# Four tiles of a product taken from the scaled input, with the norm's root multiplied in afterwards

## The reference

```python
def rmsnorm(x, g):
    xf = x.astype(jnp.float32)
    y = xf * lax.rsqrt(jnp.mean(xf * xf, axis=-1, keepdims=True) + RMS_EPS)
    return (y * g.astype(jnp.float32)).astype(x.dtype)

def modulate(h, shift, scale):
    return h * (1 + scale) + shift
...
        hx = modulate(rmsnorm(x, norm_g[l]), shift[:, None], scale[:, None])
...
def odd_mixer(h, p, on_grid):
    z = h @ p["w_in"]
    u, g = jnp.split(z, [W_POOL], axis=-1)
    d = multiscale_pool(u.reshape(bn * rows, GRID_W, W_POOL)).reshape(bn, n, W_POOL)
    d = d.reshape(bn, n, N_POOL_GROUPS, POOL_GROUP_DIM)
    y = jnp.einsum("bngi,gij->bngj", d, p["w_grp"]).reshape(bn, n, W_POOL) * p["scale"]
    return (y * jax.nn.silu(g)) @ p["w_out"]
```

## Time and profile before

| | us |
|---|---|
| median of 3 runs | 910.2 (910.13 to 910.39) |
| the profiled execution | 910.26 |
| its span in the trace | 908.5 |
| PE busy | 889.2 (98% of the span) |
| DVE busy | 700.0 (77%) |
| ACT busy | 500.7 (55%) |
| POOL busy | 142.5 (16%) |

### The profile page before, as it was taken

One profiled execution on the slowest core, in us unless ns is written; L12 is line 12 of the kernel. 1 busy time (PEld: TensorE's weight loads), 2 busy tenths in 40 slices (PEclk: granted clock), 3 DMA queues, 4 the chain that ended last, 5 costly groups with the idle time before them and its releaser, 6 DMA issues.

```text
span 908.5 us, 17445 instructions
## 1 busy us (share of the span) xinstructions
PE 889.2 (98%) x7172; PEld 834.4 (92%) x7172; DVE 700.0 (77%) x1008; ACT 500.7 (55%) x718; POOL 142.5 (16%) x254
## 2 busy tenths in 40 slices
PE   8999999999999999999999999999999999999996
PEld 7788776689999999989999999999999999999995
DVE  5689667989897999978579975797985688656553
ACT  5384888897744455325554474574444444444441
POOL 0003874800021002300211100300001000000000
PEclk9999999999999999999999999999999999999999
DMA  9946987885675777866628844555565386666661
GB/s 365 385 142 219 310 266 227 271 281 178 210 275 198 254 266 262 292 216 190 183 84 319 283 139 140 192 153 180 172 183 171 123 267 209 183 182 178 202 202 54
DMA packets 55294, 195.44 MB, mean 215 GB/s; under 512 B 7856, under 2 KB 7984, under 8 KB 53808
## 3 DMA queue, kind: packets, MB, share of 16 engines
q1 hardware_dynamic: 39600, 147.73, 50.6%
q0 software_dynamic: 15616, 46.61, 14.9%
HBM read 188.60 MB, written 1.05 MB: 209 GB/s over the span
## 4 chain that ended last, share of the span: by engine, by line
PE 76%; DVE 11%; ACT 5%; DMA 4%; issue 3%; SPq 0%; DVEq 0%; ACTq 0%
PE ps L575 22%; PE ps L577 21%; PE ps L576 21%; PE ps L736 3%; DVE w_lo L1373 3%; DMA raw<-in_stream 2%; PE px L654 2%; DMA m<-in_mod_w 2%; PE ps L665 2%; ACT w_hi L958 1%; DVE win L1387 1%; PE px L841 1%; DVE dump L1744 1%; PE px L816 1%; ACT la L1078 1%
## 5 line engine op out<-in xcount | busy, mean ns | idle before, releaser
L1373 DVE TENSOR_TENSOR w_lo<-raw,w_hi 128x1024 fp32r<-128x1024 f32 x232 | 280.5, 1226 | 103.7 <-ACT w_hi L958 103.1
L958 ACT ACTIVATE w_hi<-raw 128x1024 fp32r<-128x1024 f32 x232 | 243.2, 1056 | 116.1 <-DMA raw<-in_stream 116.0
L575 PE MATMUL ps<-h_hi,w_hi 128*128 128x256 f32 (+1 forms) x928 | 273.9, 295 | 7.1 <-DVE w_lo L1373 2.8
L576 PE MATMUL ps<-h_lo,w_hi 128*128 128x256 f32 (+1 forms) x928 | 269.5, 290 | 0.0
L577 PE MATMUL ps<-h_hi,w_lo 128*128 128x256 f32 (+1 forms) x928 | 269.3, 290 | 0.0
L575 PEld LDWEIGHTS ps<-h_hi,w_hi 128*128 128x128 f32 x928 | 177.6, 191 | 17.6 <-issue 6.4
L576 PEld LDWEIGHTS ps<-h_lo,w_hi 128*128 128x128 f32 x928 | 177.7, 191 | 3.6 <-issue 1.2
L577 PEld LDWEIGHTS ps<-h_hi,w_lo 128*128 128x128 f32 x928 | 177.7, 191 | 2.6
L452 POOL DMA_DIRECT2D modw<-in_mod_w x80 | 42.8, 537 | 384.7 <-DVE modw L1407 242.7
L575 PE MATMUL ps<-h2o_hi,w_hi 128*128 128x256 f32 x352 | 101.5, 288 | 0.0
L577 PE MATMUL ps<-h2o_hi,w_lo 128*128 128x256 f32 x352 | 99.6, 283 | 0.0
(11 more groups left out here) (336 smaller groups left out, 1759.5 us busy)
## 6 DMA issues: line engine op xcount, KB each, us to landing
raw<-in_stream SPq DMA_DIRECT2D x252, 512.0 KB, 4.0
modw<-in_mod_w POOLq DMA_DIRECT2D x80, 512.0 KB, 5.8
m<-in_mod_w SPq DMA_DIRECT2D x8, 1024.0 KB, 19.4
shifts<-upad POOLq DMA_DIRECT2D x128, 35.5 KB, 4.9
c_row<-in_c_rows SPq DMA_DIRECT2D x3, 512.0 KB, 6.3
ctxT<-in_ctxT SPq DMA_DIRECT2D x1, 1024.0 KB, 5.2
x<-in_xT SPq DMA_DIRECT2D x1, 1024.0 KB, 7.2
ctx2T<-in_ctx2T SPq DMA_DIRECT2D x1, 1024.0 KB, 6.6
```

The source lines that it names most:

```text
L575: pe.matmul(o, wh, hi, start=start, stop=False)
L576: pe.matmul(o, wh, lo, start=False, stop=False)
L958: act.activation(w_hi[split[0] % HI_RING][:], raw[n % RING][:], ACT.Copy).then_inc(w_hi_ready, 1)
L1373: v.tensor_tensor(w_lo[n % RING][:], raw[n % RING][:], w_hi[split[0] % HI_RING][:].bitcast(F32), ALU.subtract).then_inc(w_lo_ready, 1)
```

## The change

The first four `ou` tiles no longer wait for the norm. While the `yb` tiles are added to `x`, ACT makes `xa_hi` = x * scale and DVE the rest `xa_lo`, tile by tile. Two more columns of `xa` hold the shift, so a matmul is 258 wide and its column 256 gives the product with the shift. PE multiplies ou 0 to 3 by `xa` one tile after another (`thirds` in place of `side_by_side`), with the two matmuls of the sum of squares between ou 0 and ou 1, and all 18 `keep_busy` matmuls there are gone. Afterwards DVE, for each of the four tiles (`ou_root`), copies column 256 into `sums1` and multiplies the tile by the reciprocal root into `first1`; ACT adds `sums1` on the way into `opad`. ou 4 to 15 and all of `og` use `h1` as before. DVE makes `yb`'s four modulation products together, ahead of `yb` 4, runs two tiles of `w_lo` ahead of its `yb` adds in place of four from `yb` 4 on, and clears the edges of `opad` later.

```diff
--- before.py
+++ after.py
@@ -238,6 +238,9 @@
         win = [at("win0", W + 68, [16, PW]), at("win1", W + 73, [16, PW])]
         y_hi = at("y_hi", W + 78, [16, T], F32R)
         vr1 = at("vr1", W + 94, [T])
+        TS1 = T + 2
+        xa_hi, xa_lo = at("xa_hi", W + 77.75, [KT, TS1], F32R), at("xa_lo", W + 85.875, [KT, TS1], F32R)
+        first1 = at("first1", W + 12, [4, T])
         h1_hi = at("h1_hi", W + 97.25, [KT, T], F32R)
         h1_lo = at("h1_lo", W + 105.25, [KT, T], F32R)
         y_lo = at("y_lo", W + 97.25, [16, T], F32R)
@@ -362,6 +365,7 @@
         act_step = sem("act_step")
         out_done = sem("out_done")
         xg_ready = sem("xg_ready")
+        xa_rounded, xa_ready, first_ou = sem("xa_rounded"), sem("xa_ready"), sem("first_ou")
 
         modA = columns(2 * KT).rearrange("p (k w) -> p k w", w=2)
         modS = columns(2 * KT).rearrange("p (k w) -> p k w", w=2)
@@ -375,6 +379,7 @@
         ccs = columns(2 * KT)
         warm, eps_col = columns(1), columns(1)
         sc1, gate1 = columns(KT), columns(KT)
+        sums1 = columns(4)
         shift1 = columns(KT)
         lb_t = [columns(2 * HEADS) for _ in range(3)]
         lb, oml, noml = (columns(2 * HEADS) for _ in range(3))
@@ -717,13 +722,13 @@
                 thirds("yb", t, *yb, first=False)
 
 
-            keep_busy(4)
-            two_chunks(px[0], sq1, 1, KT)
-            keep_busy(14)
             h1 = (lambda k: h1_hi[:, k, :], lambda k: h1_lo[:, k, :])
-            side_by_side([("ou", t) for t in range(4)], *h1, (h_ready, 0))
+            for t in range(4):
+                thirds("ou", t, lambda k: xa_hi[:, k, :], lambda k: xa_lo[:, k, :], TS1, (xa_ready, 1) if t == 0 else None)
+                if t == 0:
+                    two_chunks(px[0], sq1, 1, KT)
             for t in range(4, 2 * KT):
-                thirds("ou", t, *h1)
+                thirds("ou", t, *h1, ready=(h_ready, 0) if t == 4 else None)
             for t in range(2 * KT):
                 thirds("og", t, *h1)
             two_chunks(px[1], sqx, 2, 2 * KT)
@@ -1188,19 +1193,25 @@
                 act.activation(dst[:, t, :], x[:, t, :], ACT.Square).then_inc(sq_ready, 1)
 
             root_table()
+            act.activation(xa_hi[:, :, T:TS1], shift1.rearrange("p (k a) -> p k a", a=1).to_broadcast([P, KT, 2]), ACT.Copy) \
+               .then_inc(xa_rounded, 1)
             for t in range(KT):
                 done("yb", t)
+                emptied(act, "yb", t)
+                act.activation(xa_hi[:, t, 0:T], x[:, t, :], ACT.Identity, scale=sc1[:, t:t + 1]).then_inc(xa_rounded, 1)
                 squares("yb", t, sq1)
+            highs("ou", 4)
 
             root_of_mean(5, vr1[:], px[0])
             shifted(0, h1_hi, t1, shift1)
+            highs("ou", 6)
             act.wait_ge(pads_ready, 1)
-            highs("ou", 5)
-            for t in range(2 * KT):
-                if t < 4:
-                    act.wait_ge(tile_done, TILE[("ou", t)] + 1)
-                else:
-                    done("ou", t)
+            for t in range(4):
+                emptied(act, "ou", t)
+                act.activation(opad[:, t, :, 8:8 + GRID_W], first1[:, t, :].rearrange("p (r c) -> p r c", c=GRID_W),
+                               ACT.Identity, bias=sums1[:, t:t + 1]).then_inc(first_ou, 1)
+            for t in range(4, 2 * KT):
+                done("ou", t)
                 act.activation(opad[:, t, :, 8:8 + GRID_W],
                                psum_of("ou", t)[:, 0:T].rearrange("p (r c) -> p r c", c=GRID_W), ACT.Copy) \
                    .then_inc(free_of("ou", t), 1)
@@ -1386,9 +1397,9 @@
             def tt_(o, a, b, op):
                 return v.tensor_tensor(o, a, b, op)
 
-            def modulate(count, src, rstd, scale, shift, tmp, hi, lo):
-
-                for s in range(KT + 2):
+            def modulate(count, src, rstd, scale, shift, tmp, hi, lo, steps=range(KT + 2)):
+
+                for s in steps:
                     if s < KT:
                         v.scalar_tensor_tensor(out=tmp[:, s, :], in0=src[:, s, :], scalar=scale[:, s:s + 1], in1=rstd,
                                                op0=ALU.mult, op1=ALU.mult).then_inc(pre_ready, 1)
@@ -1690,17 +1701,28 @@
 
             def add_to_x(name, t, gate):
 
-                if t < KT - 1 or name == "ob":
+                if name != "yb" and (t < KT - 1 or name == "ob"):
                     ahead(name, t)
                 v.wait_ge(tile_done, TILE[(name, t)] + 1)
                 xt = x[:, t, :]
                 v.scalar_tensor_tensor(out=xt, in0=psum_of(name, t)[:, 0:T], scalar=gate[:, t:t + 1],
                                        in1=xt, op0=ALU.mult, op1=ALU.add).then_inc(free_of(name, t), 1)
 
+            v.wait_ge(xa_rounded, 1)
+            v.tensor_tensor(xa_lo[:, :, T:TS1], shift1.rearrange("p (k a) -> p k a", a=1).to_broadcast([P, KT, 2]),
+                            xa_hi[:, :, T:TS1].bitcast(F32), ALU.subtract).then_inc(xa_ready, 1)
             for t in range(KT):
+                if t == 4:
+                    lows("yb", 4)
+                    mod_tiles(7, 1)
+                    lows("yb", 5)
                 add_to_x("yb", t, gate0)
-                if t < 4:
-                    mod_tiles(7, 1, t, 1)
+                if t < KT - 1:
+                    ahead("yb", t, 4 if t < 4 else 2)
+                emptied(v, "yb", t)
+                v.wait_ge(xa_rounded, t + 2)
+                v.scalar_tensor_tensor(out=xa_lo[:, t, 0:T], in0=x[:, t, :], scalar=sc1[:, t:t + 1],
+                                       in1=xa_hi[:, t, 0:T].bitcast(F32), op0=ALU.mult, op1=ALU.subtract).then_inc(xa_ready, 1)
 
             def rstd(n, t, dst):
 
@@ -1710,10 +1732,26 @@
 
 
             lows("ou", 3)
+            rstd(4, vr1[:], vr1[:])
+
+            def ou_root(t):
+
+                v.wait_ge(tile_done, TILE[("ou", t)] + 1)
+                S.do(v.tensor_copy(sums1[:, t:t + 1], psum_of("ou", t)[:, T:T + 1]))
+                S.sync()
+                v.tensor_tensor(first1[:, t, :], psum_of("ou", t)[:, 0:T], vr1[:], ALU.mult).then_inc(free_of("ou", t), 1)
+
+            ou_root(0)
+            modulate(0, x, vr1[:], sc1, shift1, t1, h1_hi, h1_lo, range(4))
+            lows("ou", 4)
+            modulate(0, x, vr1[:], sc1, shift1, t1, h1_hi, h1_lo, range(4, KT + 2))
+            ou_root(1)
+            lows("ou", 5)
+            ou_root(2)
+            ou_root(3)
             S.do(v.memset(opad[:, :, :, 0:8], 0.0))
             v.memset(opad[:, :, :, 8 + GRID_W:PW], 0.0).then_inc(pads_ready, 1)
-            rstd(4, vr1[:], vr1[:])
-            modulate(0, x, vr1[:], sc1, shift1, t1, h1_hi, h1_lo)
+            lows("ou", 6)
             v.wait_ge(pads_ready, 1)
 
             def window(g):
@@ -1760,6 +1798,8 @@
 
             def pooled(g):
 
+                if g == 0:
+                    v.wait_ge(first_ou, 4)
                 for t in range(4 * g, 4 * g + 4):
                     emptied(v, "ou", t)
                 total = window(g)
```

## The result

The changed kernel takes 917.33 us (median of 5, 916.2 to 924.1) against 910.2: a ratio of 1.0082 (95% interval 1.0056 to 1.0108), so 7 us slower. A second series of the same kernel gave 917.45 (12 runs, 915.66 to 924.03) against 910.98 (35 runs, 909.39 to 917.78) for the kernel before, a ratio of 1.0069 (1.0045 to 1.0093), 6.5 us. The forecast was 916.8 within 914.4 to 918.6.

A forecast was written before the change was run, and what follows sets the result against it. DVE's unbroken work from the last add through `w_lo` of ou 7 sets the pace: 6.5 us added, less 0.7 idle, plus 0.8 for the clock makes 6.6 us slower, 916.8 us (914.4 to 918.6).

The forecast's parts named there:

- PE at the border: Between yb 7 and ou 0: ou 0 starts 6.3 us earlier without a wait; seen from PE alone, a 5.3 us gain.
- The yb adds cost nothing: Ahead of the border: extra `xa_lo` and four modulation products in a row cost nothing, covered by PE's 14.4 us.
- Four `ou_root`, 3.1 us: On DVE behind the last add: four copy-and-multiply pairs at 0.77 us each, from a range of 0.55 to 0.85.
- DVE's sum: Work added on DVE between the last add and `w_lo` of ou 7: 6.5 us (5.5 to 6.8).
- The idle time ahead of the second window sum goes: DVE's 0.73 us idle ahead of `pooled(1)` vanishes, so ou 10 starts 6.5 - 0.7 = 5.8 us later.
- The clock, 0.8 of 0.2 to 1.4: PE's clock falls in the wait ahead of ou 7, which starts at half rate: 0.8 us reach the path.
- Waits of 1.5, 0.6 and 8.6: PE's waits for `w_lo`: about 1.5 us for ou 5, 0.6 for ou 6 and 8.6 for ou 7.
- Nothing comes back later: Between 345 and 900 us, later waits take up none of the delay: 0 given back, at best 0.3 us.
- The sum: Whole kernel: 5.8 + 0.8 = 6.6 us slower; profiled execution 916.9 us, median 916.8 us.
- PE's gain arrives: Rival: PE's 5.3 us gain at the border reaches the end, giving 904.9 us; chance 3%.
- DVE's path alone, no clock term: Rival: clock stays at 2.4 GHz through the wait ahead of ou 7 or rises at once; 916.0 us; chance 24%.
- It doesn't do what it says: Rival: `xa_lo` comes late and ou 0 waits, and the root with it; about 918 us; chance 3%.

The follow-up runs named there:

- small-parts runs: Kernel before with four products together ahead of yb 4 and zeros later: 915.42 us; with the yb-adds part whole, `w_lo` behind each add, zeros unmoved: 914.0 us.
- run with ones: Changed kernel with 34 matmuls on ones put ahead of ou 7, where PE waits: 917.06 us, ratio 1.0064.
- runs with room on DVE: Four second pairs out of ou, POOL's sums earlier, `h2c` modulated in small pieces, some `w_lo` earlier: changed kernel 905.73 us, kernel before 909.31 us.
- run with three pairs: Changed kernel with three second pairs taken out of the ou stage, later pairs three places back into og and grp: 913.84 us, ratio 1.0023.
- run with five pairs: Five second pairs moved from ou to later stages, `h2c` modulated whole between adds of ob 3 and 4: changed kernel 923.25 us, kernel before 922.06 us.

## Why the prediction was right, step by step

- *PE at the border.* Right: ou 0 at 281.72 (said 281.8), no wait ahead of it, the sums at 284.60 (284.7).
- *The yb adds cost nothing.* Right for the change: last add at 281.93, PE's border at 281.72. The small-parts runs show how narrow it is: the same products with the `w_lo` ahead of the adds, and the zeros moved, cost 5 us.
- *`w_lo` of ou 1 and 2, 2.3 us.* Right, and seen by itself: 2.27.
- *`xa_lo` of tile 7, 1.1 us.* Right: 1.2 measured (282.33, where the add gives way, to 283.52).
- *Four `ou_root`, 3.1 us.* This term of the sum was mis-sized, by the prediction's own sign ("the copies take other than 0.37"). A root is 0.52 to 0.54 (288.70 to 289.24 above), 2.1 in all, below my lower bound of 0.55. I took 0.37 from the copy to the product, from two operations of which one needs the other's result, and 0.40 for the product. Measured: 0.20 (288.70 to 288.90) and 0.34 (288.90 to 289.24). The sync behind the copy, for which I leaned to the upper end, costs hardly more than the 0.14 of a pair without a wait.
- *DVE's sum.* 5.53 instead of 6.5, all of the miss in the roots.
- *The idle time ahead of the second window sum goes.* Wrong in the letter: 0.81 us are left. It goes at full clock, as the run with ones shows (no wait, DVE there at 317.81). The slow ou 7 brings it back, so this is the same 0.9 us that stood in my next term.
- *The clock, 0.8 of 0.2 to 1.4.* Right: it fell in the wait, and costs 0.9. It rose after some 18 matmuls 0.21 apart, three quarters of ou 7. The price I took from the program's start, 0.221 against 0.117, stood on a weak row: the profile's clock column reads 1.00 there (1.3 to 6.6 us), so that row doesn't show the lower level. ou 7's own rows do, 0.21 at 0.50 against 0.12 at 1.00, and the size is nearly the same. The rule that I weighed there (the Trainium skill, "TensorE: Matmul & The Clock Gate", section "Why this matters for your kernels") holds in mid-program for this wait of 8.30 us by this trace; shorter ones didn't all behave alike (last section).
- *Waits of 1.5, 0.6 and 8.6.* Measured 1.04, 0.36 between two starts, 8.30: each a little less, by the shorter roots.
- *Nothing comes back later.* Right: og 3, oa (416.81 against 411.19) and f behind its first tile (467.90 against 462.22) are all 5.6 to 5.7 later.
- *The sum.* Said 6.6 in the trace; at f it is 5.7. The rest of the 6.6 between the two profiled executions (916.86 - 910.26) is 0.55 in a wait for `m_lo` at 687.76 (1.28 against 0.73 before; the run with ones has 0.64, so it isn't the change) and 0.4 outside the span (2.16 against 1.76). The roots, 1.0 too dear, and these two, 0.95 that no term had, cancel in the profiled execution; the medians of the two series, 7.1 and 6.5 us apart, can't tell them from each other. The time was met partly by luck, the mechanism not.

Of the rivals, *PE's gain arrives* needed less than 0.7 us of added work on DVE and got 5.5; the runs with room on DVE show it as real at 3.6 us. *DVE's path alone, no clock term* is refuted by the clock's rows and the 0.9 us of the run with ones. *It doesn't do what it says* is refuted by ou 0 at 281.72.

## What to carry to other kernels

A hole in the busiest engine is worth filling only if the engine that feeds it can keep up with the head start: take the chain of waits across the hole, and price the change on the engine that the chain runs on, PE at 98% or not. If that engine is full, count what may move off it, and give it a place where it idles in small pieces of known length. Here two steps behind each of five adds cost PE no wait, and the same modulation as one block between two adds cost it 5.24 us. Before moving work, look at what is queued behind its loads on the issuing queue, and at how many steps now stand in a row ahead of one that others wait for.

## What I had not expected of the hardware

The clock can fall in a much shorter wait than the one of 8.3 us. In the run with three pairs it was at 0.99 up to 432.2 and at 0.50 from there, after 2.62 us without a matmul. Ahead of ou 7 the same run had a wait of 1.91 us and no fall (the next matmuls are 0.12 apart). The run with five pairs had one of 1.90 there, and the clock fell, not in the wait but 0.8 us behind its end, with PE at work again:

```profile
306.50:308.30 1.80, 0.00 (x0) 0.00 (x0) 1.80 (x3) 1.80 (x4) 0.00 (x0) 1.00 0.49 112
308.40:310.00 1.60, 1.60 (x10) 1.60 (x11) 1.60 (x2) 1.11 (x2) 0.00 (x0) 0.76 0.51 205
310.00:312.00 2.00, 2.00 (x12) 2.00 (x11) 0.60 (x1) 0.00 (x0) 0.00 (x0) 0.50 0.00 0
```

So two waits of the same length had two outcomes, and the length alone doesn't tell.

DVE's steps are longer while POOL adds. In the kernel before, the same product takes 1.75 us beside POOL's sums of squares, which end at 368.2, and 1.21 behind them (DVE's timeline):

```profile
365.91 1.75 DVE L1744 SCALAR_TENSOR_TENSOR dump<-modw,c_row 128x1024 f32<-128x1024 f32 x1
...
370.41 1.21 DVE L1744 SCALAR_TENSOR_TENSOR dump<-modw,c_row 128x1024 f32<-128x1024 f32 x1
```

The Trainium skill, "GPSIMD Engine Reference", section "Specifications", says that the two engines share their interface to the buffer memory, with contention when a DVE instruction has two inputs there, as this one has; the rows agree. Whoever moves work on a full DVE may want to keep it clear of such stretches; no run here tried that by itself.
